# An fp32 router by column halves and smaller routing tables in a two-layer mixer and MoE trunk

## What is computed

```
x  = x + concat(y_a, y_b, y_c) @ w_out[l]
h2 = rmsnorm(x, norm2_g[l])
x  = x + hier_moe(h2, ...)

g_prob = softmax(t @ rg_w + rg_b);  g_sel = argmax(g_prob)          # 4 groups
e_in   = (t @ re_w + re_b) of the chosen group                      # 4 experts each
top_v, top_i = top_k(softmax(e_in), 2);  top_v /= sum(top_v)
y_t    = sum over the two experts: p_g * top_v * ((silu(t @ w_gate) * (t @ w_up)) @ w_down)
```

## Time and profile before

| | us |
|---|---|
| median of 3 runs (1225.26 to 1230.44) | 1228.84 |
| profiled execution | 1230.1 |
| its span, first to last instruction | 1228.3 |
| TensorE busy / VectorE busy / ScalarE busy | 1161.0 / 1011.6 / 741.3 |
| mean granted TensorE clock | 0.984 of full |

### The profile page before, as it was taken

One profiled execution on the slowest core, in us unless ns is written; L12 is line 12 of the kernel. 1 busy time (PEld: TensorE's weight loads), 2 busy tenths in 40 slices (PEclk: granted clock), 3 DMA queues, 4 the chain that ended last, 5 costly groups with the idle time before them and its releaser, 6 DMA issues.

```text
span 1228.3 us, 17892 instructions
## 1 busy us (share of the span) xinstructions
PE 1161.0 (95%) x5920; PEld 925.2 (75%) x5920; DVE 1011.6 (82%) x1611; ACT 741.3 (60%) x1054; POOL 118.2 (10%) x156
## 2 busy tenths in 40 slices
PE   5999998998999999999899999999999999999995
PEld 4866875786788888888677578658687888888874
DVE  4998986347699999999769799852668999999995
ACT  5234248432688888888542432771527888888882
POOL 5100000001011110110400000000000111011131
PEclk9999999999999999999999999999989999999997
DMA  9722211118899999999753122112479999999985
GB/s 305 273 92 74 87 35 35 64 41 324 270 392 394 393 391 393 393 393 365 181 190 121 52 86 69 35 36 86 169 257 320 381 393 391 394 392 393 391 250 158
DMA packets 145565, 290.36 MB, mean 236 GB/s; under 512 B 17104, under 2 KB 19216, under 8 KB 145472
## 3 DMA queue, kind: packets, MB, share of 16 engines
q1 hardware_dynamic: 130176, 237.63, 54.1%
q0 software_dynamic: 15296, 51.55, 12.6%
HBM read 263.41 MB, written 25.69 MB: 235 GB/s over the span
## 4 chain that ended last, share of the span: by engine, by line
PE 68%; DVE 8%; ACT 4%; issue 2%; DMA 1%; POOL 1%; ACTq 0%; DVEq 0%; POOLq 0%
PE ps L381 19%; PE ps L383 19%; PE ps L382 19%; PE ps L599 3%; DVE w_lo L373 2%; PE ps L733 2%; PE ps L855 1%; ACT w_hi L369 1%; PE ps L841 1%; PE ps L752 1%; PE ps L818 1%; DVE x_sb L1336 1%; DVE x_sb L1354 1%; PE ps L865 1%; DMA arena<-y_rows,yidx 1%
## 5 line engine op out<-in xcount | busy, mean ns | idle before, releaser
L369 ACT ACTIVATE w_hi<-raw 128x1024 fp32r<-128x1024 f32 (+1 forms) x256 | 268.1, 1053 | 208.9 <-PE ps L383 203.9
L381 PE MATMUL ps<-w_hi,a_hi 128*128 128x512 f32 x960 | 381.8, 398 | 11.5 <-DVE w_lo L373 10.6
L383 PE MATMUL ps<-w_hi,a_lo 128*128 128x512 f32 x960 | 376.0, 392 | 0.0
L382 PE MATMUL ps<-w_lo,a_hi 128*128 128x512 f32 x960 | 375.9, 392 | 0.0
L373 DVE TENSOR_TENSOR w_lo<-raw,w_hi 128x1024 fp32r<-128x1024 f32 (+1 forms) x256 | 302.6, 1209 | 81.4 <-ACT w_hi L369 72.9
L373 DVE TENSOR_TENSOR w_lo<-arena,w_hi 128x1024 fp32r<-128x1024 f32 x192 | 227.8, 1220 | 9.6 <-ACT w_hi L369 0.9
L369 ACT ACTIVATE w_hi<-arena 128x1024 fp32r<-128x1024 f32 x192 | 203.6, 1063 | 43.8 <-PE ps L383 38.4
L381 PEld LDWEIGHTS ps<-w_hi,a_hi 128*128 128x128 f32 x960 | 181.4, 189 | 50.3 <-issue 11.8
L383 PEld LDWEIGHTS ps<-w_hi,a_lo 128*128 128x128 f32 x960 | 181.3, 189 | 38.5
L382 PEld LDWEIGHTS ps<-w_lo,a_hi 128*128 128x128 f32 x960 | 181.6, 189 | 35.8
L381 PE MATMUL ps<-a_hi,w_hi 128*128 128x512 f32 (+1 forms) x304 | 121.4, 400 | 5.5 <-DVE a_lo L1381 4.2
(11 more groups left out here) (248 smaller groups left out, 1214.1 us busy)
## 6 DMA issues: line engine op xcount, KB each, us to landing
arena<-in_w_down SPq DMA_DIRECT2D x144, 256.0 KB
raw<-in_w_gate SPq DMA_DIRECT2D x136, 256.0 KB, 2.6
raw<-in_w_up SPq DMA_DIRECT2D x136, 256.0 KB, 2.9
arena<-in_w_gate SPq DMA_DIRECT2D x120, 256.0 KB
arena<-in_w_up SPq DMA_DIRECT2D x120, 256.0 KB
raw<-in_w_down SPq DMA_DIRECT2D x112, 256.0 KB, 9.4
raw<-in_w_in SPq DMA_DIRECT2D x80, 256.0 KB, 6.0
y_rows<-arena POOLq DMA_DIRECT2D x42, 256.0 KB, 5.8
```

Of the source, the lines that this page charges most:

```text
L369: nc.scalar.activation(split_slot(w_hi, n, w), place(S, i, n, w), ACT.Copy).then_inc(S.w_hi_set, 1)
L381: nc.tensor.matmul(o, lh, rh, start=start, stop=False)
L382: nc.tensor.matmul(o, lh, rl, start=False, stop=False)
L383: return nc.tensor.matmul(o, ll, rh, start=False, stop=stop)
```

## The change

- Transposes: the blocks of row tiles 0 and 1 go to banks 0 to 3 (two column blocks to a bank), those of 2 and 3 to banks 4 to 7. `norm_copy` takes the place of `norm_hi` and `norm_lo` in this norm: plain fp32 copies of the banks, six on ScalarE and two on VectorE.
- Router: 16 fp32 products of 256 columns in place of the 24. Even column blocks of the 1024 go to output rows 0 to 63, odd ones to 64 to 127, two token halves, four banks. Each half is copied once it is done, rows 0 to 63 by ScalarE, 64 to 127 by VectorE; four fp32 products with a selection matrix (C_SEL) add the two row halves and turn them token-major. The split of rw is gone.
- Routing: `e2k` and `p2k` stay raw; the overflow arithmetic leaves `route`. A hot row has 32 columns, 16 with token numbers and 16 with gates, made ahead of the positions; after the positions only the 8 one-hots of the rank are made (`slots`). 8 products give both tables.
- Spins: 20 instead of 10 ahead of the positions, 4 instead of 12 behind them, none between table products, 17 behind them in place of 12 and 4.
- `extras` (number of extra tiles, their experts, yidx for the main gathers) follows the tables on VectorE; `over_rows` and `over_tables` stand in the branch for extra tiles. `yc_in` has one semaphore for each row tile.

```diff
 def norm_transposes(k):
+    for tt in range(TT):
+        half, odd = divmod(tt, 2)
...
+            bank = 4 * half + c // 2
+            at = (c % 2) * HALF + odd * P
+            mm = T.transpose(ps[:, bank, at:at + P], hrow[:, tt, c * P:(c + 1) * P], ident)
+            if odd and c % 2:
                 mm.then_inc(ht_ready, 1)
 def router(l):
-    for c in range(DC):
-        mm = three(ps[0:20, 0, :], rw_hi[:, l, c, :], rw_lo[:, l, c, :], a_hi[:, c, :], a_lo[:, c, :], ...)
-    mm.then_inc(rlog_ready, 1)
-    pe.wait_ge(lgt_set, l + 1)
+    for half in range(2):
+        for q in range(4):
+            pe.wait_ge(ht_hi, 14 * l + 8 + (4 if half else max(q + 1, 2)) + (min(q + 1, 2) if half else 0))
+            if half and q >= 2:
+                pe.wait_ge(ht_lo, 10 * l + 8 + q - 1)
+            for d in range(2):
+                at = (l * DC + 2 * q + d) * 20
+                mm = T.matmul(ps[d * 64:(d + 1) * 64, 2 * half + d, 0:HALF], rw_flat[:, at:at + RW_COLS],
+                              hT[q][:, d, half * HALF:(half + 1) * HALF], start=q == 0, stop=q == 3)
+        mm.then_inc(rlog_ready, 1)
+    pe.wait_ge(lgt_set, 4 * (l + 1))
     for tt in range(TT):
-        mm = T.transpose(ps[:, 1, tt * 32:tt * 32 + 20], lgT[0:20, tt * P:(tt + 1) * P], ...)
+        mm = T.matmul(ps[:, 4, tt * 32:tt * 32 + 20], lgT[:, tt * P:(tt + 1) * P], cst[:, C_SEL:C_SEL + 20], ...)
-    spin(7, 10)
+    spin(7, 20)
...
-    spin(7, 12)
+    spin(7, 4)
     for q in range(TT * TOPE):
-        spin(7, 1)
+        mm = T.matmul(ps[:, 3, 0:2 * E], slot_hot[:, q, :], R["hot"][:, q, :], ...)
     mm.then_inc(tab_ready, 1)
-    spin(7, 12)
-    for q in range(TT * TOPE):
-        mm = T.matmul(ps[:, 4, 0:TILES], slot_hot[:, q, :], R["hot"][:, q, :], ...)
-    mm.then_inc(tab_ready, 1)
-    spin(7, 4)
+    spin(7, 17)
+    pe.wait_ge(tab_set, 2 * (l + 1))
+def norm_copy(k):                                   # ScalarE; VectorE has (1, 2) and (1, 3)
+    for half, q in ((0, 0), (0, 1), (0, 2), (0, 3), (1, 0), (1, 1)):
+        sc.wait_ge(ht_ready, DC * k + 4 * half + q + 1)
+        A.copy(hT[q][:, :, half * HALF:(half + 1) * HALF], ps[:, 4 * half + q, :]...).then_inc(ht_hi, 1)
 def route(l):
-    V.tensor_tensor(gates[:, 1, :], gates[:, 0, :], R["fe"], ALU.mult)
+    link(V.tensor_tensor(gates[:, 1, :], gates[:, 0, :], R["fe"], ALU.mult))
+    V.tensor_tensor(hot[:, :, :, 0:E], R["m12"], cst[:, C_TOK:C_TOK + TT]..., ALU.mult)
+    link(V.tensor_tensor(hot[:, :, :, E:2 * E], R["m12"], gates[:]..., ALU.mult))
     ve.wait_ge(pos_ready, l + 1)
+    link(V.tensor_tensor(R["tm"], here, R["m12"], ALU.mult))
+    link(V.tensor_reduce(R["p2"], R["tm"], AX, ALU.add))
+    slots()
+    ve.wait_ge(tab_ready, l + 1)
+    V.tensor_copy(tab[:, 0:E], ps[:, 3, 0:E]).then_inc(tab_set, 1)
+    V.tensor_copy(gslot[:, 0:E], ps[:, 3, E:2 * E])
+    V.tensor_copy(R["count"], ps[:, 2, TT * E:(TT + 1) * E]).then_inc(tab_set, 1)
...
 norm_rows(2 * l + 1, lambda tt: add_mixed(l, tt))
-norm_lo(2 * l + 1)
+norm_copy(2 * l + 1)
 lo(ve, main, None, n0 + PIECES_IN + 11)
 route(l)
+extras(l)
```

More of the change, by code:

```diff
@@ L199, in trunk @@
         zeros = ar(A_SC, D)
-        lgT = ar(A_P, SEQ)
+        lgT = ar(A_O, SEQ)
+        hT = [ar(at, 1024, 2, SEQ) for at in (A_V, A_V + 1024, A_P, A_L)]
         diag = ar(A_P, P)
@@ L267, in trunk @@
         h2_stored = sem("h2_stored")
-        yc_in = [sem(f"yc_in{q}") for q in range(TT * TOPE)]
+        yc_in = [sem(f"yc_in{tt}") for tt in range(TT)]
         ysum_ready, late_add = sem("ysum_ready"), sem("late_add")
@@ L1197, in _ @@
                 hi(sc, main, None, n0 + PIECES_IN + 11)
-                norm_hi(2 * l + 1)
-                sc.wait_ge(rlog_ready, l + 1)
-                A.copy(lgT[0:20, :], ps[0:20, 0, :]).then_inc(lgt_set, 1)
+                norm_copy(2 * l + 1)
+                for half in range(2):
+                    sc.wait_ge(rlog_ready, 2 * l + half + 1)
+                    A.copy(lgT[0:64, half * HALF:(half + 1) * HALF], ps[0:64, 2 * half, 0:HALF]).then_inc(lgt_set, 1)
                 for q in range(2):
@@ L1339, in add_late @@
             def add_late(l, tt):
-                for k in range(TOPE):
-                    ve.wait_ge(yc_in[TOPE * tt + k], 16 * (l + 1))
+                ve.wait_ge(yc_in[tt], 32 * (l + 1))
                 V.tensor_tensor(x[:, tt, :], late_rows[tt], x[:, tt, :], ALU.add).then_inc(late_add, 1)
@@ L1484, in route @@
                 ve.wait_ge(pos_ready, l + 1)
                 here = ps[:, 2, 0:TT * E].rearrange("p (t e) -> p t e", t=TT).unsqueeze(1).to_broadcast(by_expert)
-                count = ps[:, 2, TT * E:(TT + 1) * E]
-                V.tensor_tensor(R["tm"], here, R["m12"], ALU.mult)
-                link(V.tensor_scalar(R["ex"], count, 128.0, None, ALU.is_gt))
-                for q in (256.0, 384.0):
-                    link(V.scalar_tensor_tensor(out=R["ex"], in0=count, scalar=q, in1=R["ex"], op0=ALU.is_gt, op1=ALU.add))
@@ L1522, in route @@
-                link(V.scalar_tensor_tensor(out=R["d2"], in0=R["b2"], scalar=float(-ZERO_ROW), in1=R["d2"], op0=ALU.add, op1=ALU.mult))
-                V.tensor_scalar(yidx[:, 0], R["c2"], float(ZERO_ROW), None, ALU.add)
-                V.tensor_scalar(yidx[:, 1], R["d2"], float(ZERO_ROW), None, ALU.add)
-                for k in range(TOPE):
-                    for tt in range(TT):
-                        ins = V.scalar_tensor_tensor(out=R["hot"][:, TT * k + tt, :], in0=cst[:, C_IOTA:C_IOTA + TILES],
-                                                     scalar=e2k[:, k, tt:tt + 1], in1=gates[:, k, tt:tt + 1].to_broadcast([P, TILES]),
-                                                     op0=ALU.is_equal, op1=ALU.mult)
```

179 lines of the change are left out of this document (108 added, 71 removed).

## The result

The changed kernel has a median of 1219.09 us (1218.47 to 1221.01, 4 runs); the kernel before, with one more run beside it, 1227.79 us (1225.26 to 1230.44, 4 runs). The profiled execution took 1221.01 us (span 1219.2), 9.1 less than that of the kernel before.

A forecast was written before the change was run, and what follows sets the result against it. TensorE was taken to wait for VectorE's chain between the second norm's transposes and the first expert product. Rows 9.2 us earlier, less 1.6 for clock, gave -7.6 on 1228.84: 1221.2 us, own range 1218 to 1224.5, 8 in 10 from 1214.5 to 1226.5.

The forecast's parts named there:

- What bounds the kernel: Between the second norm's last transposes and the first expert product TensorE waits for VectorE's chain; a stage starting earlier ends earlier.
- Transposes to logits: Router stretch in each layer: 8 pairs of fp32 products at 0.49 us replace 24 products; logits 1.9 us earlier.
- The rival that they do not overlap: Router products in column pairs take 6.9 us instead of 3.9, costing at most 6.0 over two layers: 1227.2 us; chance 0.12.
- Logits to table: Routing chain without overflow arithmetic: token table 9.45 us after the logits in both layers, 4.05 us gained.
- The 2.2 us for layer 1's slow stretch: Ahead of layer 1's token table: changed unread products close the idle and shorten the queue, gaining 2.2 us besides.
- Gather: Token table to expert rows: the gather, issued earlier at full DMA share, lands after 7.2 us, bounds 4.2 and 8.0.
- the fourth rival: Weight queue, refilled from 300.5 by the earlier extras, starves the gather; at 15 us landing 1236.7 us; chance 0.03.
- 3.5 and 5.7 us: Gathered rows reach TensorE earlier by 3.5 us in layer 0 and 5.7 us in layer 1, 9.2 together.
- Clock: TensorE idles some 3.9 us per layer before the rows; one loss by lower clock counted net over two layers, 1.6 us.
- The rival that the clock stays low: Idle wait for the gather brings half clock in both layers, 6.4 us lost instead of 1.6: 1226 us; chance 0.10.
- Costed at nothing: Extras (2.4 us of VectorE) under the gather, removed rw split, yc_in waits and overflow rows: taken as no time.
- Sum: Whole execution: -9.2 for earlier rows plus 1.6 for the clock, -7.6 us, from 1228.84 to 1221.2 us.

## Why the prediction was right, and where it was not

- **What bounds the kernel**: right. Rows that come 4.2 and 7.8 us earlier gave a last sum 9.1 us earlier.
- **Transposes to logits**, 1.9 us: measured 2.3 in both layers. The pairs took 0.459 us where 0.49 was taken, and the last of them needed no 0.25 more to end (3.67 in all for 3.9 + 0.25). The rival that they do not overlap fell: 7.12 us without pairs, 3.67 with them. The Trainium skill's rule on row groups (TensorE: Matmul & The Clock Gate, "The mechanism"), as the prediction applied it to column halves, would have had 6.9 us for the pairs; the trace disagrees.
- **Logits to table**, 9.45 us in both: 10.21 and 9.67. Every stretch of this kind at full clock took 9.66 to 9.68, so the estimate was 0.2 short; layer 0 has 0.55 on top, since the clock fell to 0.50 ahead of its table. There 20 and 4 unread products did not hold it, as again with 23 waits (9.97). The 2.2 us for layer 1's slow stretch were exact, as the kernel before with 18 unread products shows (15.68 to 13.49).
- **Gather**, 7.2 us from issue to rows: 7.8 and 8.1, at the upper bound of 8.0. The reason given, the backlog of the 28 pieces, is shown by holding 4 of them back (4.4 us in layer 0). The other one named, SyncE resuming earlier, adds 0.5 us at most; with it falls what was left of the fourth rival. The step "3.5 and 5.7 us" came out, less what each layer inherited, at 2.6 and 5.0: 0.9 and 0.7 short, of which the landing time is 0.6 and 0.9.
- **Clock**, one net loss of 1.6 us: from rows to last silu the stage went from 278.4 to 280.0 in layer 0 and from 280.0 to 279.4 in layer 1, a net loss of 0.9. The size of one loss, read from the earlier trace rows, was right (1.6); the term was nearly twice too large because in layer 1 the half clock behind the wait for the gather took the place of the one at the stall, at 0.9. The idle wait was 1.7 us in layer 0, since its 17 products ran at half clock, and 4.7 in layer 1, where 3.9 were said for each. The rival that the clock stays low fell.
- **Costed at nothing**: no loss appears in the chain of landmarks where the extras, the split of rw or the yc_in waits stand; they were not tried one by one. What was missed is that the *code* itself has a price: the move of instructions shifts the stall behind the branch. In the change the tail came out at -0.6 us (30.8 to 30.2), by luck, a second stop of 2.3 us in place of 3.1 us lost to half clock; elsewhere tails lie between -3.2 and +6.1 of the kernel before.
- **Sum**: -7.6 predicted, -9.1 in the profile, -8.7 between the medians. The stretch that was forecast gave 7.6 us (2.6 and 5.0) where 9.2 were said, and the clock cost 0.9 where 1.6 were said; so the terms of the sum come to -6.7. The rest of the profile's -9.1 was not in the sum: 1.6 from the attention stage's clock, 0.6 from the tail and 0.2 between the layers. That the total hit the forecast so well is in part luck.
- **What each part is worth** was not foreseen. The old tables with the new router and 8 more unread products have the time of the whole change (0.9935), with a last silu 1.1 us later and a tail 2.6 shorter. The removed overflow chain brings the table forward by 3.5 and 3.6 us against that kernel, but the rows by only 0.5 and 0.6, since the gather then stands in the queue.

## What to carry to other kernels

When a chain ends in a DMA, look at what stands in the queues at the new time of its issue: here some three of eight microseconds went to a backlog, and holding four weight pieces back until the gather was on its way was worth 0.4% more, with and without the added waits, at no cost to the stage that uses them. Before judging a variant by its time alone, read the tail behind each branch: a variant can look slower by 0.7% for where its code lies, and a few waits that are always met tell that from a fault of its own.

## What the runs showed of the hardware

- A gather of 128 rows issued by POOL takes 4.4 us from issue to use in layer 0 and 5.9 in layer 1 with four 512 KB pieces fewer ahead of it, and 7.8 and 8.1 behind the whole backlog of weight pieces at a DMA share of 1.04 to 1.05; with the queue in that state an earlier issue is not an earlier landing.
- TensorE stood idle behind a branch with its data ready for 0.7 to 4.7 us in six kernels and for some 6 of its 9.0 us in a seventh; 23 added waits moved the tail by -9.2 us in one kernel and by +5.2 in another. In all seven TensorE goes on 14.6 to 16.0 us behind the last silu.
- fp32 products in different column halves overlap fully: 0.459 us a pair, 0.445 for a single one of 256 columns.
- The same instructions of the attention stage ran at a mean granted clock of 0.66, 0.83 or 1.00 (180 to 190 us), although the code ahead of them was the same (0.66 before and 0.83 before with 18 products; 0.83 changed and 1.00 with 34 unread products), and the last transposes of layer 0 came up to 3.3 us apart. The runs do not settle why.
